# The first memory's key product laid into the norm ahead of the first MLP of a two-block transformer kernel

## The reference

```python
x = x + gate1 * (merged @ w_out)
h2 = rmsnorm(x, g_norm2) * (1.0 + scale2) + shift2
x = x + gate2 * (jnp.square(jax.nn.relu(h2 @ w_mlp1)) @ w_mlp2)
return rmsnorm(x, g_final)
...
mem_n = rmsnorm_2(mem, mem_norm)
# in layer l
kv = jnp.einsum('bmd,de->bme', mem_n, w_mem_kv[l])
k = rmsnorm_2(kv[..., :256] by heads of 64, k_gain)   # v is the other 256 columns
qh = rmsnorm_2(q of the layer's input by heads, q_gain)
sc = einsum('bshd,bmhd->bhsm', qh, k) * 64 ** -0.5, softmax, times v
```

## Time and profile before

| | us |
|---|---|
| median of 3 runs | 1117.15 (1115.64 to 1118.68) |
| the profiled execution | 1116.6 |
| its span | 1114.8 |
| PE busy in it | 1067.2 (96%) |
| DVE, ACT, POOL busy | 644.7, 545.5, 373.9 |
| mean granted clock of TensorE | 0.983 of full speed |
| DMA | 197.39 MB, 177 GB/s on average |

### The profile page before, as it was taken

How to read it: one execution, slowest core, us unless ns; L and a number is a source line. 1 busy time by engine, 2 the same in 40 slices (tenths; PEclk the granted TensorE clock), 3 DMA queues, 4 the chain that set the end, 5 groups by cost and what they waited for, 6 DMA issues and landing times.

```text
span 1114.8 us, 19839 instructions
## 1 busy us (share of the span) xinstructions
PE 1067.2 (96%) x8566; PEld 1046.3 (94%) x8566; DVE 644.7 (58%) x834; ACT 545.5 (49%) x770; POOL 373.9 (34%) x198
## 2 busy tenths in 40 slices
PE   6889999999999999989999999999999989999998
PEld 6889999999999999989999999999998779999998
DVE  3857756665775554635855454445857656544443
ACT  3357866633556434563335354443754544443341
POOL 2436257231464532452021352222331411352221
PEclk9989999999899999999999999999999999999999
DMA  9987748536377555524355555556533215655541
GB/s 324 288 269 234 221 126 293 187 115 190 112 256 260 177 178 189 189 96 133 114 189 190 189 189 189 180 179 200 154 121 100 77 45 183 227 177 176 178 151 39
DMA packets 173957, 197.39 MB, mean 177 GB/s; under 512 B 5380, under 2 KB 146093, under 8 KB 173741
## 3 DMA queue, kind: packets, MB, share of 16 engines
q1 hardware_dynamic: 173868, 196.11, 54.5%
HBM read 195.03 MB, written 1.06 MB: 176 GB/s over the span
## 4 chain that ended last, share of the span: by engine, by line
PE 83%; DVE 5%; ACT 3%; POOL 2%; DMA 2%; issue 2%; SPq 2%; DVEq 1%; ACTq 0%; POOLq 0%
PE bank L502 82%; DMA ada_raw<-in_w_ada 2%; DVE w_lo L1743 1%; ACT w_hi L1185 1%; SPq L458 1%; POOL ada_raw L1593 1%; DMA probsT<-in_buckets 1%; POOL stat L1705 1%; ACT ada_raw L1175 1%; PE bank L757 0%; POOL head_bias L1628 0%; DVE y_tok L2285 0%; DVE big L2154 0%; ACT h_hi L1222 0%; ACT big L1234 0%
## 5 line engine op out<-in xcount | busy, mean ns | idle before, releaser
L1743 DVE TENSOR_TENSOR w_lo<-w_raw,w_hi 128x2048 fp32r<-128x2048 f32 x158 | 385.8, 2445 | 244.7 <-ACT w_hi L1185 243.6
L502 PE MATMUL bank<-h_hi,w_hi 128*128 128x256 f32 x1328 | 378.7, 290 | 11.8 <-DVE w_lo L1743 7.6
L502 PE MATMUL bank<-h_hi,w_lo 128*128 128x256 f32 x1328 | 373.4, 286 | 0.0
L1185 ACT ACTIVATE w_hi<-w_raw 128x2048 fp32r<-128x2048 f32 x158 | 301.4, 1909 | 129.3 <-PE bank L502 121.6
L502 PE MATMUL bank<-h_lo,w_hi 128*128 128x256 f32 x1328 | 347.8, 285 | 1.2 <-POOL h_lo L1561 1.2
L502 PE MATMUL bank<-u_hi,w_hi 128*128 128x256 f32 x1024 | 290.9, 287 | 4.1 <-ACT u_hi L1194 2.7
L502 PE MATMUL bank<-u_hi,w_lo 128*128 128x256 f32 x1024 | 288.6, 285 | 0.0
L1561 POOL TENSOR_TENSOR u_lo<-fresh,u_hi 128x512 fp32r<-128x512 f32 x60 | 142.4, 2375 | 402.1 <-ACT u_hi L1194 402.0
L502 PE MATMUL bank<-u_lo,w_hi 128*128 128x256 f32 x1024 | 277.1, 284 | 0.0
L502 PEld LDWEIGHTS bank<-h_hi,w_hi 128*128 128x128 f32 x1328 | 259.9, 196 | 17.5 <-DVE w_lo L1743 9.4
L502 PEld LDWEIGHTS bank<-h_hi,w_lo 128*128 128x128 f32 x1328 | 259.8, 196 | 0.0
(11 more groups left out here) (247 smaller groups left out, 1023.1 us busy)
## 6 DMA issues: line engine op xcount, KB each, us to landing
w_raw<-in_w_mlp SPq DMA_DIRECT2D x32, 1024.0 KB, 5.4
w_raw<-in_w_up SPq DMA_DIRECT2D x32, 1024.0 KB, 5.4
w_raw<-in_w_down SPq DMA_DIRECT2D x32, 1024.0 KB, 5.1
w_raw<-in_w_in SPq DMA_DIRECT2D x21, 1024.0 KB, 6.0
ada_raw<-in_w_ada SPq DMA_DIRECT2D x19, 1024.0 KB, 7.9
w_raw<-in_a_w_in SPq DMA_DIRECT2D x10, 1024.0 KB, 5.2
w_raw<-in_w_o SPq DMA_DIRECT2D x8, 1024.0 KB, 5.0
w_raw<-in_w_out SPq DMA_DIRECT2D x4, 1024.0 KB, 4.9
```

The costliest lines, as they stand in the source:

```text
L502: return pe.matmul(dst, lhsT, rhs, start=start, stop=stop, skip_group_check=True)
L1185: act.activation(w_hi[:, n % PARTS_RING, :], w_raw[:, slot_of[n], :], ACT.Copy).then_inc(hi_w, 1)
L1743: dve.tensor_tensor(w_lo[:, n % PARTS_RING, :], w_raw[:, slot_of[n], :], w_hi[:, n % PARTS_RING, :].bitcast(F32), ALU.subtract).then_inc(l ...
```

## The change

The key unit of the first memory moves from behind the first MLP to the front of it and becomes unit 30 (`N_M0K`). The MLP's units become 31 to 62, the value unit stays 63 (`N_M0V`). The key product uses the memory times its gain only, without the root of its rows ("unrooted"). ScalarE and VectorE make its hi and lo parts in `u_hi` and `u_lo` while the `w_out` units run. The root cancels in the norm by heads if its epsilon is scaled by the memory's mean square, which the new `mean_mem` writes (`mem_eps`). PE does the unit in three pieces of 18, 12 and 18 matmuls (`mem_key`), ahead of and behind the last sum of squares and behind the spread. In the norm, VectorE no longer adds the shift: ScalarE adds it while it makes `h_hi` (an Identity with a bias), and VectorE makes `h_lo` with the shift in one instruction per tile, which GpSimd did before. The MLP's first `product_two` does the first two pairs of its first unit ahead (`early=2`), that of the query unit all four (`early=4`).

The diff's core (line numbers that only shift, and names, are left out):

```diff
-ADA_LATE = {**{2 + 2 * i: ADA_FIRST + i for i in range(12)}, **{32 + 4 * i: 20 + i for i in range(4)}}
+ADA_LATE = {**{2 + 2 * i: ADA_FIRST + i for i in range(12)}, **{33 + 4 * i: 20 + i for i in range(4)}}
...
+    mem_unit(0, "k", 0)
     mlp("mlp0", w["w_mlp1"], w["w_mlp2"])
-    mem_unit(0, "k", 0)
     mem_unit(0, "v", MEM_W)
...
 (PE)
+            def mem_key(first, last):
+                n = N_M0K
+                if first == 0:
+                    pe.wait_ge(m0_lo, 4)
+                    start_unit(n)
+                for at in range(first, last):
+                    nt, kt = at // KT, at % KT
+                    for i, (w, x) in enumerate(((wh, u_hi), (wh, u_lo), (wl, u_hi))):
+                        ins = mm(...)
+                if last == 2 * KT:
+                    ins.then_inc(unit_done, 1)
             add_squares(2, 2)
+            mem_key(0, 6)
             add_squares(2, 3)
-            pe.wait_ge(fresh_ready, J_H2)
+            mem_key(6, 10)
             spread_sum(2, ps_ada)
+            mem_key(10, 16)
...
-            mlp(N_MLP0, J_H2, J_MLP0, between={6: sum_mem, 7: spread_mem}, ready=(fresh_hi, fresh_lo))
+            mlp(N_MLP0, J_H2, J_MLP0, early=2, between={6: sum_mem, 7: spread_mem}, ready=(fresh_hi, fresh_lo))
             pe.wait_ge(mem_lo_done, 4)
-            product(N_M0, mem_hi, mem_lo)
-            product_tok(N_M0 + 1, mem_hi, mem_lo)
-            product_two(N_QM0, h_hi, h_lo, in_order(X_H4), ready=(x_hi, x_lo))
+            product_tok(N_M0V, mem_hi, mem_lo)
+            product_two(N_QM0, h_hi, h_lo, in_order(X_H4), early=4, ready=(x_hi, x_lo))
...
 (ACT)
+            split_w(N_OUT + AHEAD)
+            act.wait_ge(unit_done, N_BR + 4)
             for i in range(4):
-                split_w(N_OUT + i + AHEAD)
+                act.wait_ge(mem_in[i // 2], 16)
+                for k in (2 * i, 2 * i + 1):
+                    last = act.activation(u_hi[:, k, :], mem_pair[i][...], ACT.Copy, scale=vec[:, V_MEM + k:V_MEM + k + 1])
+                last.then_inc(m0_hi, 1)
+            for i in range(4):
+                if i:
+                    split_w(N_OUT + i + AHEAD)
                 act.wait_ge(xt_ready, i + 1)
                 square_pair(2, i, flat(xT, 2 * i, 2 * i + 2))
+            split_w(N_M0K + AHEAD)
             for q in range(4):
-                split_h(J_H2 + q, h_hi, 2 * q)
+                act.wait_ge(fresh_ready, J_H2 + q + 1)
+                for i in range(2):
+                    k = 2 * q + i
+                    last = act.activation(h_hi[:, k, :], fresh[:, q % 2, i * T:i * T + T], ACT.Identity, bias=ada[:, 24 + k:25 + k])
+                last.then_inc(fresh_hi, 1)
+            evac_qk("mem0", N_M0K, flat(mem_k0, 0, 2), mem_squares)
...
 (ACT, behind the first MLP)
-            split_w(N_QM0)
+            split_w(N_QM0 + 1)
+            evac(N_M0V, flat(mem_v[:, 0], 0, 2))
             squares_x("sum3")
-            evac_qk("mem0", N_M0, flat(mem_k[:, 0], 0, 2), mem_squares)
-            split_w(N_QM0 + 1)
             squares_x("sum3g")
-            evac(N_M0 + 1, flat(mem_v[:, 0], 0, 2))
...
 (POOL)
             power("sum2")
-            for q in range(4):
-                split_h(J_H2 + q, h_lo, h_hi, 2 * q)
...
 (DVE)
             for i in range(4):
                 n = N_OUT + i
-                if i < 3:
-                    split_w(n + AHEAD)
+                split_w(n + AHEAD)
+                dve.wait_ge(m0_hi, i + 1)
+                for k in (2 * i, 2 * i + 1):
+                    last = dve.scalar_tensor_tensor(out=u_lo[:, k, :], ...)
+                last.then_inc(m0_lo, 1)
                 dve.wait_ge(unit_done, n + 1)
...
-            split_w(N_OUT + 3 + AHEAD)
             mean_square("sum2")
             dve.wait_ge(spread_full, spread_no["sum2"] + 1)
-            normed(J_H2, gs[:, 1, :], ps_ada, ada[:, 24:32])
+            normed_h2(0)
+            normed_h2(1)
+            split_w(N_M0K + AHEAD)
+            shifted_lo(0)
+            normed_h2(2)
+            shifted_lo(1)
+            normed_h2(3)
+            shifted_lo(2)
+            shifted_lo(3)
...
-            mean_square("qk.mem0")
+            mean_square("qk.mem0", mem_eps)
```

More of the change, by code:

```diff
@@ L325, in two_blocks @@
         mem_squares = flat(big, 12, 14)
+        mem_k0 = qk[:, 0:2, :]
+        mem_eps = stat[:, 86:88]
         x_hat = qk
@@ L354, in two_blocks @@
             "mem_sq", "mem_summed", "mem_normed", "mem_hi_done", "mem_lo_done"))
+        m0_hi, m0_lo = sem("m0_hi"), sem("m0_lo")
         consts_in, vec_in, x_in, small_in = (sem(s) for s in ("consts_in", "vec_in", "x_in", "small_in"))
@@ L950, in _ @@
             pe.wait_ge(qk_normed, k_no["qk.mem0"] + 1)
-            attention("mem0.", 2, lambda g: qi[:, g, :], lambda g: mem_k[:, 0, g, :],
+            attention("mem0.", 2, lambda g: qi[:, g, :], lambda g: mem_k0[:, g, :],
                       lambda h, s: mem_v[:, 0, s, h * HD:h * HD + HD], FULL_BLOCKS, FULL_SPAN,
@@ L2033, in _ @@
                 n = N_OUT + i
-                if i < 3:
-                    split_w(n + AHEAD)
+                split_w(n + AHEAD)
+                dve.wait_ge(m0_hi, i + 1)
+                for k in (2 * i, 2 * i + 1):
+                    last = dve.scalar_tensor_tensor(out=u_lo[:, k, :], in0=mem_pair[i][:, (k % 2) * T:(k % 2) * T + T],
+                                                    scalar=vec[:, V_MEM + k:V_MEM + k + 1], in1=u_hi[:, k, :].bitcast(F32),
+                                                    op0=ALU.mult, op1=ALU.subtract)
+                last.then_inc(m0_lo, 1)
                 dve.wait_ge(unit_done, n + 1)
@@ L2040, in _, with normed_h2, shifted_lo @@
                                                     scalar=ada[:, 16 + k:17 + k], in1=xT[:, k, :], op0=ALU.mult, op1=ALU.add)
-                    if j == 0:
-                        continue
-                    last.then_inc(evac_v, 1)
+                last.then_inc(evac_v, 1)
                 dve.drain().then_inc(xt_ready, 1)
-            split_w(N_OUT + 3 + AHEAD)
             mean_square("sum2")
-            dve.wait_ge(spread_full, spread_no["sum2"] + 1)
-            normed(J_H2, gs[:, 1, :], ps_ada, ada[:, 24:32])
+            def normed_h2(q):
+                dst = fresh_slot(J_H2 + q)
+                for i in range(2):
+                    k = 2 * q + i
+                    last = dve.scalar_tensor_tensor(out=dst[:, i * T:i * T + T], in0=xT[:, k, :], scalar=gs[:, 1, k:k + 1],
+                                                    in1=ps_ada[:, 0:T], op0=ALU.mult, op1=ALU.mult)
+                last.then_inc(fresh_ready, 1)
+            def shifted_lo(q):
+                dve.wait_ge(fresh_hi, J_H2 + q + 1)
+                for i in range(2):
+                    k = 2 * q + i
+                    last = dve.scalar_tensor_tensor(out=h_lo[:, k, :], in0=fresh[:, q % 2, i * T:i * T + T],
+                                                    scalar=ada[:, 24 + k:25 + k], in1=h_hi[:, k, :].bitcast(F32), op0=ALU.add,
+                                                    op1=ALU.subtract)
+                last.then_inc(fresh_lo, 1)
+            dve.wait_ge(spread_full, spread_no["sum2"] + 1)
+            normed_h2(0)
[7 more added lines that the diff above has]
+            shifted_lo(3)
             rstd_read()
@@ L2090, in mlp, with mean_mem @@
                         last.then_inc(xt_ready, 1)
+            def mean_mem():
+                from_misc("summem")
+                at = root_at["summem"]
+                link(dve.tensor_scalar(root[:, at:at + 2], ps_misc[:, 0:2], 1.0 / D, EPS, ALU.mult, ALU.add))
+                dve.tensor_scalar(mem_eps, root[:, at:at + 2], EPS, None, ALU.mult).then_inc(misc_read, 1)
             def normed_mem():
@@ L2101, in normed_mem @@
                 dve.drain().then_inc(misc_read, 1)
-            mlp(N_MLP0, ada[:, 40:48], {6: lambda: mean_square("summem"), 7: normed_mem})
+            mlp(N_MLP0, ada[:, 40:48], {6: mean_mem, 7: normed_mem})
             for q in range(4):
                 split_x(X_H4 + q, q, h_hi, h_lo, V_MIX)
-            split_w(N_QM0)
             split_w(N_QM0 + 1)
@@ L2128, in _ @@
                 last.then_inc(xt_ready, 1)
-            qk_scale("mem0", flat(mem_k[:, 0], 0, 2), V_MK, acc[1])
+            qk_scale("mem0", flat(mem_k0, 0, 2), V_MK, acc[1])
             split_w(N_CONV + 2 + AHEAD)
```

9 lines of the change are left out of this document (7 added, 2 removed).

## The result

The changed kernel takes **1121.74 us** (median of 6 runs, 1120.13 to 1123.40), the kernel before 1117.2 (6 runs, 1115.21 to 1118.68): ratio 1.0043, 95% interval 1.0029 to 1.0057. It is slower by 0.4%, a little more than the bound of 0.3%. The forecast was 1122.0, with 1118 to 1125. The profiled execution is 1120.13, its span 1118.3, against 1116.6 and 1114.8. In what follows *before* and *after* are the two kernels, and *fill* is the key product laid into the norm.

The account below looks back on a forecast made before the run. PE, busy for 96% of the span, was taken to bound the kernel. The terms 5.4 - 0.2 - 0.5 + 0.2 = +4.9 us on 1116.6 gave 1121.5, with 0.55 for the median 1122.0 us, range 1118 to 1125.

Parts of the forecast that it names:

- Step 1: Before the norm: squares form a ring of engines waiting in turn; added `u_lo` pairs put the third square at 272.35.
- Step 2: Last addition to `xT` behind a split and the last `u_lo`: PE idles 3.5 us to 277.9, last square at 278.8.
- Step 3: Fill and chain before the norm: clock falls after 1 us idle, VectorE's first pair comes at 285.2 (283.0 to 285.6).
- S: The time of VectorE's first pair in the norm, forecast 285.2, before at 279.23.
- Step 4: Norm: PE idles 5.4 us until the key bank is emptied, resumes at S + 9.5, low clock costs 2.0; +5.4 us.
- Step 5: Norm: GpSimd's four `h_lo` and the shift go; nothing counted beyond Step 4.
- Step 6: Behind the MLP: query-unit idle goes, PE waits 0.9 us for sums, net -0.2 us; low clock there -0.5 us.
- Step 7: Key's mean with its own epsilon: one more VectorE instruction ahead of a split PE waits for, +0.2 us.
- the fill keeps the clock: Rival: TensorE stays at 2.4 GHz through the first gap, recovers fast after the second; +2.2 us, 1119.3; chance 17%.
- The fill works: Rival: first piece runs from 274.4, bank emptied in time, clock stays high; -8.0 us, 1109.1; chance 10%.
- point of decision: PE's start on the MLP's second unit: before 289.9 the whole is a gain, after it a loss.
- The sums collide: Rival: VectorE's split of unit 65 falls on GpSimd's first sum of x, PE waits 2.2 us longer; 1124.2; chance 11%.

Follow-up runs that it names:

- e1: After, with the memory's lo parts 1 to 3 made in VectorE's waits and unit 31's split behind the last addition to `xT`: 1118.18 us, 1.0016 of before.
- e8: After, with only the memory's lo parts moved into VectorE's waits, the split of unit 31 left in place: 1116.12 us, 1.0014 of before.
- e6: Before, with only the norm rewritten (shift in ScalarE's hi parts, lo parts on VectorE), key unit not moved: 1116.07 us, 0.9993 of before.
- e7: After, without `early=4` for the query unit's `product_two`: 1121.71 us, 1.0040 of before.
- e3: After, with both edits, lo parts in VectorE's waits and the key bank emptied between ScalarE's second and third pair: 1111.45 us, 0.9960 of before.
- e4: The kernel of e3 with the key product cut in pieces of 9, 12 and 27 matmuls instead of 18, 12 and 18: 1110.38 us, 0.9953 of before.
- e2: After, with ScalarE's emptying of the key product's bank moved from behind the fourth `h_hi` pair to behind the second: 1119.83 us, 1.0035 of before.
- e10: The unchanged kernel of e2 run once more on another chip for a second profile: 1114.06 us, beside 1117.34 for before.
- e5: The kernel of e4 with VectorE's split of unit 66 ahead of its reading of the row sums: 1109.10 us, 0.9932 of before.
- e9: The unchanged kernel of e1 run once more on another chip for a second profile: 1117.24 us, beside 1117.34 for before.

## Why the prediction was right

The mechanism was right in its steps, and the sum (+4.9 us) near the medians' +4.5; the profile's +3.5 holds a start that was 1.1 us quicker, for which no part of the change was named. That the median came out within 0.3 us is partly luck: the stage of the norm was reckoned 0.8 too high, and the terms below that go by the clock are moved by single executions by more than that.

- *Step 1, the ring:* right. One round 6.42, forecast 6.44; the third square at 271.19 + 1.12 = 272.31, forecast 272.35.
- *Step 2, the first wait:* right. 3.43 us, forecast 3.5; the last `u_lo` ended at 276.7 + 1.1 = 277.85, as forecast; the last square started at 278.73, forecast 278.8. e1 and e8 show that the place of `u_lo` is the cause.
- *Step 3, S:* 283.51 + 1.12 = 284.63, forecast 285.2, within its bounds (283.0 to 285.6). **The step that failed in size** is "the clock falls as it did before after 1 us": it fell 3.5 us after the sums and was low for 3.4, back in time for the last sum (0.95 us) and the way to the spread (2.31 us, forecast 2.6 at the low clock). That took most of the 0.6 us off.
- *Step 4, the second wait:* 5.21 us, forecast 5.4, ended by the square of the bank, as named. PE goes on 9.32 us behind S, forecast 9.5. The Identity instructions take 1.71 us for four and 0.91 for two, so 0.40 for one more and, worked out from these, 0.51 for one by itself; the row with two pointers that I used has 2.08 for four. The figure of the Trainium skill (ScalarE: Activation LUTs, "What ACT_TABLE_LOAD costs"), 493 ns, agrees better with that than the row's 0.52 plus a tail. The low clock cost 11.63 - 9.6 = 2.0 us (292.83 to 304.46 for 80 matmuls), forecast 2.0. (One of the three low stretches behind the mean of 4.6 us ended at 238.3, not 238.2, which changes nothing.) The stage: +4.63, forecast +5.4; 0.6 of the difference is step 3, 0.2 step 4.
- *Step 5:* right. Nothing, by e6.
- *Step 6:* GpSimd's sums took 4.7 us each (the first 488.69 to 493.39), undisturbed, forecast 4.75; PE waited 0.85 for them, forecast 0.9; net -0.11, forecast -0.2. The 2.97 us for unit 66 stayed. The low clock behind it was the second term mis-sized: -1.04, forecast -0.5, just past the end of its bounds. It is no gain of the change: the clock of the kernel before was low for 6.8 us there in its one profile, and e6, with the same work there, has 3.4 and 11.00 us. The forecast took the idle of 0.90 us away for `early=4`; e7 shows that without it PE stands still for 0.62 us there and then has no wait for the sums, so the stretch is as long.
- *Step 7:* right. The wait that ends with the split of the next unit is longer by what was added on VectorE ahead of that split: 0.85 us instead of 0.67 (rows below the list). That is the +0.18 of its stretch, forecast +0.2. The wait is 0.67 in e6 too, and 0.85 or 0.86 in every other run, though the instruction was not tried alone.
- *Not in the sum:* +0.92 in the stretch around the second block. PE's idle time there is 0.6 us less than before (10.93 for 11.55), its busy time 1.5 more for the same 2540 matmuls. e6 has 327.77 with the key unit where it was, e7 326.32 with it moved, so the loss goes with the execution's clock and not with the change.

The wait of step 7, of the kernel before and then of after:

```profile
510.57 0.39 PE L502 MATMUL bank<-h_hi,w_hi 128*128 128x256 f32 x1 [0.67 <-DVE w_lo L1743]
513.13 0.38 PE L505 MATMUL bank<-h_hi,w_hi 128*128 128x256 f32 x1 [0.85 <-DVE w_lo L1773]
```

Of the rivals, "the fill keeps the clock" did not come: the clock stayed high for 3.5 us in which the fill had not yet started, and fell as it did. "The fill works" did not come, and the reason given, that both waits stand in the instruction order, is shown: moving the one and the other makes the kernel faster than before. The price of that case was too high: -8.0 us was forecast, and e3 and e4 are 4.3 and 5.4 below the kernel before beside them, though e4's stage is 7.5 shorter. Its point of decision was PE's start on the second MLP unit at 289.9 on the axis of before. With each kernel's axis shifted to it by the first mark: after 293.9 (+4.63 us in the stage), e2 293.7 (+0.8), e8 289.4 (-0.1), e1 288.9 (-0.4), e3 286.1 (-6.3, with the clock kept). e10 breaks it, with 291.2 and yet -1.6: the point was reckoned with a low clock behind the second wait, and there was none. "The sums collide" did not come in after, only in e5.

## What to carry to other kernels

Independent work laid into a gap paid here only once its own last input was ready before the gap opened and its output buffer was emptied before the next user came. Look for both in the instruction order of the engines that serve it, and put the serving work where those engines wait anyway. The same fill, in the same place, made this kernel 0.4% slower with two such waits and 0.4 to 0.5% faster without them (e3, e4). Where a stage's clock falls, judge its gain by more than one profile, or split each stretch into PE's idle and busy time and compare the idle times.

## What the runs showed that was not expected

The time from PE's stop to the fall of the clock isn't constant: 1.4 us before (with the last sums begun in between), 3.5 in after, and 2.1 and 3.8 in two executions of one kernel with a wait of equal length; and the low clock then lasted 10.2 and 3.4 us. Executions of one kernel on one chip spread by up to 8.0 us (e8), and a second profile moved a single stage by 2.5. So a stage's clock cost read from one profile is a draw: in two profiles of one kernel (e1 and e9, e2 and e10) PE's waits in the norm and behind the MLP repeat to 0.02 us, their low clocks don't. These runs don't settle why the clock falls earlier in one execution than in another. It also stays open why e1's and e2's medians fell by less than their stages: the differences seen in e9 and e10 are large enough for that, but two profiles show no mean.
